# A two-block transformer kernel on one Trainium2 core: the opening, the row terms and the quadrant sums in another order

## The reference

```python
c_act = silu(c)
mod = c_act @ ada_w + ada_b                # 6 * 1024 values
sh1, sc1, ga1, sh2, sc2, ga2 = split(mod, 6)
h = rmsnorm(x, pre_mix_g) * (1 + sc1) + sh1
x = x + ga1 * rmsnorm(hybrid_mixer(h), post_mix_g)
h = rmsnorm(x, pre_ffn_g) * (1 + sc2) + sh2
x = x + ga2 * rmsnorm(swiglu_ffn(h), post_ffn_g)
```

## Time and profile before

| | before |
|---|---|
| median of three runs | 1411.0 us (1410.42 to 1411.23) |
| the profiled execution's own time | 1412.21 us |
| its span, first to last instruction | 1410.5 us |
| mean granted clock | 0.989 |
| busy share: PE, PEld | 97%, 84% |
| busy share: DVE, ACT, POOL | 71%, 50%, 10% |
| bytes moved | 147.28 MB, 104 GB/s in the mean |
| in the first of 40 slices | 362 GB/s |
| chain that ended last | PE 85%, DVE 9%, ACT 4%, issue 2% |

### The profile page before, as it was taken

How to read it: one execution, slowest core, us unless ns; L and a number is a source line. 1 busy time by engine, 2 the same in 40 slices (tenths; PEclk the granted TensorE clock), 3 DMA queues, 4 the chain that set the end, 5 groups by cost and what they waited for, 6 DMA issues and landing times.

```text
span 1410.5 us, 19633 instructions
## 1 busy us (share of the span) xinstructions
PE 1368.1 (97%) x7774; PEld 1180.7 (84%) x7774; DVE 997.4 (71%) x1383; ACT 711.7 (50%) x1153; POOL 140.2 (10%) x115
## 2 busy tenths in 40 slices
PE   8999999999999999999999999999789999999997
PEld 6888888788679999978887788887568999998885
DVE  5799898786687878785337845667777787877332
ACT  4466886643465555562225434544345555555221
POOL 2188344100100000030000000000000000000000
PEclk9999999999999999999999999999899999999999
DMA  9422112466502323316431231110121233332321
GB/s 362 153 89 91 45 46 90 135 212 221 209 16 90 120 91 118 137 45 194 134 98 67 76 104 60 46 46 16 61 89 35 101 103 107 104 122 95 100 90 60
DMA packets 41131, 147.28 MB, mean 104 GB/s; under 512 B 4560, under 2 KB 4816, under 8 KB 40912
## 3 DMA queue, kind: packets, MB, share of 16 engines
q1 hardware_dynamic: 41040, 146.03, 30.5%
HBM read 143.91 MB, written 2.10 MB: 104 GB/s over the span
## 4 chain that ended last, share of the span: by engine, by line
PE 85%; DVE 9%; ACT 4%; issue 2%; DMA 0%; POOL 0%; DVEq 0%; SPq 0%; ACTq 0%; POOLq 0%
PE ps L1601 26%; PE ps L1602 26%; PE ps L1603 26%; PE ps L1744 1%; DVE t_buf L994 1%; DVE w_lo L960 1%; PE ps L1643 1%; DVE act_lo L1244 1%; PE ps L1983 1%; ACT w_hi L495 1%; PE ps L1970 1%; PE ps L1654 1%; PE ps L1655 1%; PE ps L1659 1%; DVE h_lo L986 1%
## 5 line engine op out<-in xcount | busy, mean ns | idle before, releaser
L1601 PE MATMUL ps<-h_hi,w_hi 128*128 128x256 f32 (+1 forms) x1120 | 375.3, 335 | 4.0 <-ACT sq L721 1.1
L1602 PE MATMUL ps<-h_lo,w_hi 128*128 128x256 f32 (+1 forms) x1120 | 372.2, 332 | 0.0
L1603 PE MATMUL ps<-h_hi,w_lo 128*128 128x256 f32 (+1 forms) x1120 | 372.1, 332 | 0.0
L960 DVE TENSOR_TENSOR w_lo<-raw,w_hi 128x1024 fp32r<-128x1024 f32 x141 | 182.8, 1300 | 113.0 <-ACT w_hi L495 112.3
L1601 PEld LDWEIGHTS ps<-h_hi,w_hi 128*128 128x128 f32 x1120 | 213.1, 190 | 30.2 <-issue 6.6
L1603 PEld LDWEIGHTS ps<-h_hi,w_lo 128*128 128x128 f32 x1120 | 213.2, 190 | 20.4
L1602 PEld LDWEIGHTS ps<-h_lo,w_hi 128*128 128x128 f32 x1120 | 213.3, 190 | 19.5 <-issue 0.5
L495 ACT ACTIVATE w_hi<-raw 128x1024 fp32r<-128x1024 f32 x141 | 148.1, 1055 | 146.3 <-PE ps L1603 77.5
L950 DVE TENSOR_TENSOR w_lo<-quads,w_hi 128x1024 fp32r<-128x1024 f32 (+1 forms) x152 | 164.7, 1085 | 72.8 <-ACT w_hi L495 72.8
L495 ACT ACTIVATE w_hi<-quads 128x1024 fp32r<-128x1024 f32 (+1 forms) x152 | 144.3, 949 | 78.5 <-PE ps L1603 76.8
L1601 PE MATMUL ps<-act_hi,w_hi 128*128 128x512 f32 x352 | 137.7, 391 | 2.2 <-DVE act_lo L1244 2.1
(11 more groups left out here) (290 smaller groups left out, 2270.3 us busy)
## 6 DMA issues: line engine op xcount, KB each, us to landing
quads<-in_ffn_in SPq DMA_DIRECT2D x76, 512.0 KB, 4.4
raw<-in_ffn_out SPq DMA_DIRECT2D x44, 512.0 KB, 3.7
raw<-in_ada SPq DMA_DIRECT2D x32, 512.0 KB, 4.2
raw<-in_qk SPq DMA_DIRECT2D x25, 512.0 KB, 3.7
ada<-in_ada SPq DMA_DIRECT2D x16, 512.0 KB, 9.6
raw<-in_gates SPq DMA_DIRECT2D x16, 512.0 KB, 3.6
raw<-in_v SPq DMA_DIRECT2D x12, 512.0 KB, 3.7
raw<-in_ffn_in SPq DMA_DIRECT2D x12, 512.0 KB, 3.8
```

Source lines behind the costliest of these rows:

```text
L960: nc.vector.tensor_tensor(w_lo[SLOT[p]][:], raw[q % RAW][:], w_hi[SLOT[p]][:].bitcast(f32), ALU.subtract).then_inc(raw_used, 1)
L1601: nc.tensor.matmul(out, w[0], v[0], start=start, stop=False, **kw)
L1602: nc.tensor.matmul(out, w[0], v[1], start=False, stop=False, **kw)
L1603: return nc.tensor.matmul(out, w[1], v[0], start=False, stop=stop, **kw)
```

## The change

Four edits. First, c comes as one row; TensorE spreads it to 128 partitions with two matmuls on a row of 1/1024, and ScalarE takes Silu of the two halves out of PSUM with a scale of 1024. x comes in four transfers. Second, in the opening VectorE adds seven of the squares into `acc`, and TensorE sums `acc` and the eighth square with two matmuls in place of eight; the pair of `ada` rows comes the other way round, GpSimd's gain waits for one dot product where it waited for two, the first normalised tile stands ahead of the first weight half, and the number of fillers is another. Third, GpSimd's row terms wait for the last low half of block one's gated activations where they waited for the last product. Fourth, at the end of block two's last projection the second two quadrant sums and the fourth weight half stand behind the last square.

```diff
-            sp.dma_start(c_all[:], t["c"].partition_broadcast(P)).then_inc(c_in, 16)
-            for k in range(KT):
-                sp.dma_start(x[:, k, :], t["x"][:, k, :]).then_inc(x_tile[k], 16)
+            sp.dma_start(c_all[0:1, :], t["c"].partition_broadcast(1)).then_inc(c_in, 16)
+            for j in range(KT // 2):
+                sp.dma_start(x[:, 2 * j:2 * j + 2, :], t["x"][:, 2 * j:2 * j + 2, :]).then_inc(x_pair[j], 16)
...
-                for i in (k, KT + k):
+                for i in (KT + k, k):
                     sp.dma_start(ada0[:, i, :], t["ada"][i, :, :]).then_inc(ada_in[k], 16)
...
             for k in range(KT):
-                pool.wait_ge(ada_dots_done, 2 * k + 2)
+                pool.wait_ge(ada_dots_done, 2 * k + 1)
                 nc.gpsimd.tensor_scalar(gain[:, 0, k:k + 1], mod[:, KT + k:KT + k + 1], mod_b[:, k:k + 1],
                                         col("pre_mix_g", k), ALU.add, ALU.mult).then_inc(mod_ready, 1)
+                pool.wait_ge(ada_dots_done, 2 * k + 2)
...
-            pool.wait_ge(prod_of["ffn_in1"], FT)
+            pool.wait_ge(act_lo_of["ffn_in1"], FT)
             nc.gpsimd.memset(sel_f[:], 0.0).then_inc(consts2, 1)
...
-            act.wait_ge(c_in, 16)
-            nc.scalar.activation(c_all[:], c_all[:], ACT.Silu).then_inc(c_act, 1)
+            for n in range(2):
+                act.wait_ge(c_wide, 2)
+                nc.scalar.activation(c_all[:, SEQ * n:SEQ * (n + 1)], ps[:, C_BANK[n], :], ACT.Silu, scale=float(D))\
+                    .then_inc(c_act, 1)
             for k in range(KT):
-                act.wait_ge(x_tile[k], 16)
+                act.wait_ge(x_pair[k // 2], 16)
                 square(k, sq[k % 2][:], x[:, k, :])
...
-            dve.wait_ge(c_act, 1)
+            dve.wait_ge(c_act, 2)
...
             def first_h(k):
-                dve.wait_ge(mod_ready, 2 * k + 2)
+                dve.wait_ge(mod_ready, 2 * k + 1)
...
             def first_lo(k):
                 dve.wait_ge(th_ready, k + 1)
+                dve.wait_ge(mod_ready, 2 * k + 2)
...
+            for k in range(KT - 1):
+                add_square(k, opens=k == 0)
+            ada_dot(KT)
             ada_dot(0)
-            ada_dot(KT)
-            feed("glu", -AHEAD)
             dve.wait_ge(rstd_ready, 1)
             for k in range(KT):
                 first_h(k)
+                if k == 0:
+                    feed("glu", -AHEAD)
+                elif k + 1 < KT:
+                    ada_dot(KT + k + 1)
+                first_lo(k)
+                if k == 0:
+                    ada_dot(KT + 1)
                 if k + 1 < KT:
                     ada_dot(k + 1)
-                first_lo(k)
-                if k + 1 < KT:
-                    ada_dot(KT + k + 1)
                     feed("glu", k + 1 - AHEAD)
...
-                if m and m % 2 == 0:
+                if m in (2, 4):
                     feed("wout_b", m // 2)
...
                 if m == 3:
                     first_sums(1, 0)
-                    second_sums(1, 0)
+            feed("wout_b", 3)
+            second_sums(1, 0)
             normalise(3, 6, lambda k: col("ffn_norm_g_2", k), kept=1)
...
             pe.wait_ge(consts, 1)
-            busy(6, 12)
-            sum_squares(1)
+            busy(6, 8)
+            pe.wait_ge(c_in, 16)
+            for n in range(2):
+                nc.tensor.matmul(ps[:, C_BANK[n], :], ones_d[0:1, :], c_all[0:1, SEQ * n:SEQ * (n + 1)],
+                                 start=True, stop=True).then_inc(c_wide, 1)
+            busy(6, 20)
+            sum_over_features(1)
             pe.wait_ge(consts, 15)
+            busy(6, 8)
+            pe.wait_ge(rstd_ready, 1)
             busy(6, 6)
-            pe.wait_ge(rstd_ready, 1)
+            pe.wait_ge(t_ready, 1)
+            busy(6, 6)
+            pe.wait_ge(th_ready, 1)
             busy(6, 4)
-            pe.wait_ge(t_ready, 1)
-            busy(6, 3)
```

More of the change, by code:

```diff
@@ L223, in build @@
         ada_in = [sem(f"ada_in{k}") for k in range(KT)]
-        x_tile = [sem(f"x_tile{k}") for k in range(KT)]
+        x_pair = [sem(f"x_pair{j}") for j in range(KT // 2)]
         raw_used, hi_ready, panel_used, ada_dots_done = (sem("raw_used"), sem("hi_ready"), sem("panel_used"),
@@ L228, in build @@
                                                           sem("lam_in"), sem("out_done"))
+        c_wide = sem("c_wide")
         c_act, consts, consts2, tri_ready, sel_ready = (sem("c_act"), sem("consts"), sem("consts2"),
@@ L284, in build @@
         K3_AT = [8, 9, 10, 11, 4, 5, 6, 7]
+        C_BANK = [4, 5]
         QK1_BANK = [0, 1, 2, 3, 4, 5, 6, 7]
```

## The result

The changed kernel takes 1404.2 us (median of five runs, 1401.9 to 1406.3), the kernel before on the same chip 1411.2. The ratio is 0.9948, with a 95% interval of 0.9937 to 0.9959: 7.3 us less, between 5.8 and 8.9. The forecast was 1403.5 us. The profiled execution is the fastest of the five, 1401.9 us with a span of 1400.2: it lies 2.3 us under the median, where that of before lay 1.0 over its own (1412.2 against 1411.2). The two traces are thus 10.3 us apart where the medians are 7.0 apart, and the 3.3 us between must not be explained as work of the change.

What follows compares the result with a forecast made beforehand. TensorE, busy 97% of the span, was taken as the bound, so only its waits and slow clock counted. Opening 0.8, row terms 3.2 and tail 3.5 sum to 7.5 us off the 1411.0 median: 1403.5 us, range 1400.8 to 1407.0.

Steps and rivals of the forecast that it cites:

- Opening: Start of the kernel: 2.0 us gained without a clock fall, 0.4 with one; 0.8 taken.
- With a fall: Opening: clock falls behind the 2.3 us gap ahead of the square sum; sum ends about 16.3, first product at 22.4.
- Eight fillers at 0.39 us: Opening: TensorE's first eight fillers end at 4.2 us, so c, landing at 4.5, comes just behind them.
- 1.6 us for its fall: Old opening: low clock after its gaps loses half of 3.3 us of work, which the new opening gives back.
- Row terms: Block one's down projection: 4.2 us saved less a 1.0 us stall, gain 3.2, between 2.5 and 4.2.
- at the pace that they imposed on the lo halves: Down projection, panel 4: GpSimd's selects slow VectorE from 0.61 for one to 3.07 us for two; half done about 640.2.
- the full stall: Panel 4 of block one's down projection: TensorE waits 1.1 us for VectorE's weight half, slowed by GpSimd.
- Tail: End of block two's last projection: sum starts 1.9 us earlier, full clock saves another 1.6; gain 3.5 us.
- Rival A: Block two's tail: the clock falls there too, 1.6 us less gain, 1405.1 us; chance 0.2.
- B: No stall at panel 4 and no clock fall in the opening: gain 9.7 us, 1401.3 us; chance 0.2.
- C: Row terms stall as much as before, now behind weight halves and their transfers: 1406.7 us; chance 0.05.
- D: Opening: c lands late, at 15.6 us, and everything behind it waits; loss 11.1 us, total 1414.6; chance 0.02.

Runs made afterwards that it cites:

- tail alone: Kernel before with only the end of block two's last projection changed (two quadrant sums and fourth weight half behind the last square): 1408.5 us against 1411.4.
- row terms alone: Kernel before with only GpSimd's row terms moved behind block one's last low half: 1407.8 us against 1411.4.
- the change twice: The changed kernel itself, unaltered, run and profiled once more on the chip of other follow-ups: 1404.1 us, ratio 0.9943 to the kernel before.
- the opening alone: Kernel before with only the opening's part of the diff: 1410.9 us against 1411.4.
- the half put back: Changed kernel with the fourth weight half of block two's last projection made at the seventh tile again, quadrant sums still behind: 1404.1 us.
- the selects twice: Changed kernel with GpSimd's four selects done twice, 8 in all: 1404.6 us, ratio 0.9952 to the kernel before.
- fewer fillers: Changed kernel with 18 fillers behind the opening's square sum in place of 24: 1403.7 us, ratio 0.9946 to the kernel before.
- three times the one-row matmuls: Changed kernel with the pair of one-row matmuls that spread c done three times: 1408.4 us.
- full rows: Changed kernel with spreading matmuls reading all 128 rows of c's tile (127 zero), c's transfer behind x's first pair: 1403.6 us, ratio 0.9940 to the kernel before.
- full rows three times: Changed kernel with the pair of spreading matmuls reading all 128 rows of c's tile (127 zero) and done three times: 1405.6 us.
- squares first with full rows: Changed kernel with ScalarE's squares ahead of the Silu, 18 fillers and spreading matmuls over 128 rows: 1402.3 us, ratio 0.9930 to the kernel before.

## Why the prediction was right, and where a term was off

The total, 1403.5, is 0.7 us under what was measured, inside the range; the forecast's own span of 1402.3 to 1404.8 holds it (the lower end of its terms, 0.4 + 2.5 + 3.5, gives 1404.6 and holds it too). That the total is so close is in part luck, for two terms were off in opposite directions. Its terms, one by one:

- **Opening, 0.8 taken between 0.4 and 2.0.** Alone 0.1 us (1.0 lost to 1.4 gained): the interval holds the 0.8, and zero as well. To see it another way, take the start of the attention row in each trace. The old opening gives 238.08 (before), 236.54 (tail alone) and 239.36 (row terms alone), the new one 236.15 and 239.13 (the change twice), 236.48 (the opening alone), 238.03 (the half put back) and 236.16 (the selects twice): means of 238.0 and 237.2, 0.8 apart, from too few executions to say more. The chain held: c in time, sum at 13.7, gap 2.3 where the fillers ran at full clock; the first product at 21.13 without a fall (20.8 forecast) and at 22.61 with the fall behind the gap (22.4 forecast). Three steps failed. "With a fall" was thought of behind the gap only; half pace also came inside the fillers, by a fall at 8 us or by a start that stayed slow until 14, and there it ate the gap. "Eight fillers at 0.39 us" end at 4.7 and not at 4.2: they run at half pace, 0.46 each, and the mean over twelve hid it; c's arrival was early enough that nothing followed from it. And the working had the old opening always pay 1.6 us for its fall; in one of three traces it paid nothing. So the worth of the opening is a draw by the clock on both sides, not 2.0 or 0.4.
- **Row terms, 3.2 taken: 4.2 less a stall of 1.0.** The 4.2 is exact in three traces (124.55 against 128.74); alone the part measured 3.1 (1.4 to 4.8), which can't tell 3.2 from 4.2. The stall didn't come in any of them. The step that failed is "at the pace that they imposed on the lo halves": a factor of 2.5 measured on 512 columns was carried to 1024, where the extra 0.9 us per instruction makes it 1.7. Three instructions at 0.9 more still end 0.4 us ahead of TensorE, and even doubled selects opened no gap. By the traces this term was 1.0 us too small. By the Trainium skill (GPSIMD Engine Reference, the table of the engine) VectorE's instructions with two SBUF inputs contend with GpSimd; the trace agrees that they do, the dot product too, but the full stall argued from it is not there. By the Trainium skill (Trainium Architecture — The Big Picture, "What this means for kernel authors") the shared port is "an exclusive lock (not a bandwidth split)". The trace agrees in that the wait comes once per instruction: 0.9 us more at both lengths in a row of instructions, and less for those that began later. The lock itself no row shows.
- **Tail, 3.5 taken.** 3.4 in the trace, gap 1.38 for 1.4, the moved work covered by 1.1 us (0.8 forecast). Alone 3.1 (1.8 to 4.4). Rival A did not occur in eleven traces. The quadrant sums bring 2.6 and the weight half 0.8.
- **Rivals B to D.** B's absence of a stall was right; its 2.0 us in the opening showed in the pair of profiles (1.9) and not in the medians. C is refuted by the 4.2 us of the row terms. D is refuted by the spreading matmuls, which start at 4.69 with no wait for c.
- **The sum.** With the terms as measured, 0.1 + 4.2 + 3.4 = 7.7 or, by the medians of the parts, 7.0; measured 7.3 (5.8 to 8.9). The forecast's 7.5 lies between because the missing stall (1.0 more) and the smaller opening (0.7 less) cancel.

What stays open: how often each opening meets a fall. That needs the distribution over many executions, and a trace shows one.

## What to carry to other kernels

Compare two profiled executions only after their place among the runs is known: here one lay above its median and one below, and their difference held 3.3 us that wasn't the change's. Where engines contend, ask of the rows whether the extra time is per instruction or in proportion, with two sizes, before carrying it to a third. Read what an edit in an opening is worth from a point behind the whole opening: the first product came 0.7 us earlier with fewer fillers, and the attention row didn't. In a serial opening at a clock that may fall, an edit that moves single microseconds is worth about what the fall's moment is worth, and only part-by-part runs of several rounds can tell.

## What the runs showed of the hardware

- TensorE's granted clock fell to 0.50 without a gap. In the change's trace TensorE was busy without a gap from 1.04 us on and the clock was down from 8.0 to 11.4; with three times the one-row matmuls it was down for 10 us.
- The recorded clock isn't the pace at a kernel's start. In all fourteen traces the first fillers took about 0.46 us each, against 0.23 later, under a recorded 1.00; in the kernels with fewer fillers and with the half put back this lasted to about 14 us.
- Gaps of the same length are followed by a fall or not. 1.86 us ahead of block two's last mean square was followed by one in the trace of before and by none in the one after. 2.34 us ahead of the opening's sum was followed by one in the second profile of the change and by none in the opening alone; 2.54 us by one with full rows and by none with full rows three times. 2.15 (the half put back) and 2.60 us (squares first with full rows) had none.
- Beside GpSimd's selects VectorE's instructions took 0.9 us more each when they followed one another, at 512 and at 1024 columns alike; later ones that began after a wait took 0.2 to 0.5 more.
- The change profiled twice had its first product at 20.77 and at 22.61 us. By the Trainium skill (TensorE: Matmul & The Clock Gate, Part 1) the moment of the clock's change isn't tied to the kernel's start and differs from run to run; these two traces agree.
